# A two-layer hybrid mixer on one core: the output tiles of the local and latent attention are turned two jobs behind their products instead of one

## The chip, the cores and the metric

The kernel runs on one core of one Trainium2 chip. The metric is the time of the device in microseconds (us) for one execution; lower is better. The median of three runs stands for a kernel.

Engines are named as in the profile: PE is TensorE (the matrix engine; PEld is its loading of weights), DVE is VectorE, ACT is ScalarE, POOL is GpSimd, SP is SyncE. PSUM is the memory that PE writes its products to, in eight banks; the program calls it `ps`.

## The reference, cut to what matters

Two layers over 512 latent tokens and 256 context tokens of width 1024. Each layer multiplies the normed tokens by one wide matrix, runs four token mixers side by side (local attention "a", an mLSTM "b", latent attention "c", differential attention "d"), and merges them by gates:

```python
def merge_branches(ys, gate_logits, w_branch, w_out):
    g = jax.nn.sigmoid(gate_logits.reshape(gate_logits.shape[:2] + (N_BRANCH, D_MODEL)))
    merged = sum(g[:, :, i] * (y @ w_branch[i]) for i, y in enumerate(ys))
    return merged @ w_out
```

The local attention has 8 heads of width 64, a window of 128 tokens on either side and the context; the latent attention has 4 heads of width 128 and sees all tokens. In both, per block of 128 query tokens and per head:

```python
p_win, p_ctx = joint_softmax([jnp.where(valid, score(qg, k_win), -jnp.inf), score(qg, k_c)], sink_f)
return values(p_win, v_win) + values(p_ctx, v_c)
```

A gated feed-forward network closes each layer. In the second layer only the latent tokens are still needed.

## The kernel before

The program is one long sequence of phases; each engine has its own stream of instructions, written by hand, and semaphores join them. Most phases are big matrix products in which every weight and every activation is split in a high and a low part (`w_hi`, `w_lo`, `u_hi`, `u_lo`), so that three matmuls stand for one.

**An attention phase** (`attend`, once for PE, once for ACT, once for DVE) works through a list of jobs. A job is one block of 128 query tokens and one head; a token block is called a tile, and its jobs follow one another: 8 in "a", 4 in "c" and "d". The first layer has 6 tiles and the second 4. Job `i` goes: scores on PE (L1433, L1439, masks L1447; written for two jobs at a time in "a" and "c", at odd `i`); maxima on DVE (L2742, L2745 or L2748); exponentials on ACT (L2032, L2034); the probabilities are transposed on PE (`probs_t`, L1467) into banks 4 and 5; ACT copies bank 4 out (L2045) and DVE bank 5 (L2784); the product with the values on PE (`values`, L1481); and DVE scales its result into `y_tok` (`y_copy`, L2795).

**Turning an output tile** (`tile_t`, L1493): when all heads of a tile are in `y_tok`, PE transposes its four 128x128 blocks into bank 4, the bank that the transposed probabilities use too. ACT then copies the bank to `y_hi` (`yt_copy`, L2070; L2068 in "d"), and DVE writes the rest to `y_lo` (`yt_low`, L2732; L2729 in "d"). Until that is done, the next `probs_t` may not write bank 4:

```python
if n.yt:
    pe.wait_ge(yt_copied, n.yt)
```

**Filling**: between these steps PE works on the product of another matrix (the gates' weights), whose matmuls are L1404: three for each 128x128 block of weights, 384 columns wide in the first layer and 512 in the second. They are what PE does while it would wait. How many stand in each job is a table written by hand (`FillPlan`; first of each pair for the first layer, second for the second layer). Of it, the local and the latent attention:

```python
THREE, FOUR, LONG = [8, 8, 8], [6, 6, 6, 6], [12, 12, 24]
"a": (3 * THREE + [12, 6, 6] + THREE + [6, 6, 12] + 2 * THREE + [6, 12, 6] + 2 * THREE + [12, 6, 6] + THREE +
      [6, 6, 12] + THREE + [4, 4],
      2 * FOUR + [5, 9, 5, 5] + FOUR + [5, 9, 5, 5] + FOUR + [5, 9, 5, 5] + [5, 4, 4]),
"c": ([24, 12, 12, 12, 12, 24] + LONG + [24] + THREE + [24] + LONG + [24] + THREE + [24, 16],
      [14, 10, 12, 12, 10, 14] + THREE + [14, 10, 7, 7, 10, 16]),
```

In "a" and "c", an odd job `i` runs on PE as: scores of `i+1` and `i+2`, values of `i-1`, perhaps a turn, all of its fill, `probs_t(i)`. An even job runs as: half of its fill (rounded down), values of `i-1`, perhaps a turn, the other half, `probs_t(i)`. In "d" every job is of the first kind, with one job's scores. The fill's chunks of 24 matmuls use bank 7 one after the other, and ACT evicts each (L2018). The weights of the fill are split while the jobs run (L2007 on ACT, L2717 on DVE).

Of the kernel before, what the change touches and what calls it, by code (L numbers as in the profile page):

```python
# [324 lines left out]
def build(nc, x, c, ctx_in, c_ctx, w_mod, b_mod, g_mix_pre, g_mix_post, g_ffn_pre, g_ffn_post, w_in, a_sink,  # L325
# [4 lines left out]
    with stack:  # L330
# [578 lines left out]
        def _(pe):  # L909
# [501 lines left out]
            def attend(l, kind, g):  # L1411
# [84 lines left out]
                    n.yt += 1  # L1496

                map0, job0 = n.map, n.job
                late = 2 if kind == "d" else 1
                scores(0)  # L1500
                for i in range(len(jobs)):
                    final = i + 1 == len(jobs)
# [119 lines left out]
            for index, (kind, l, arg) in enumerate(phases):  # L1622
                if kind == "gemm":
                    gemm(arg, background.get(index))
                elif kind == "opening":
                    opening(phases[index + 1][2][0])
                    continue
                elif kind == "close":
                    close(l, arg, phases[index + 1][2])
                    continue  # L1630
                elif kind.startswith("prep_"):
                    transposes(v_blocks(kind, l))
                elif kind == "mlstm":
                    mlstm(l, arg)
                elif kind == "attend":
                    attend(l, *arg)
                onward = kind in ("gemm", "mlstm", "attend") and phases[index + 1][0] in ("gemm", "close")
                ph.end_products(onward)
# [3 lines left out]
        def _(act):  # L1642
# [347 lines left out]
            def attend(l, kind, g):  # L1990
# [80 lines left out]
                    n.yt += 1  # L2071

                yt0 = n.yt
                late = 2 if kind == "d" else 1
                yt_tiles = [jobs[i][0] for i in range(heads - 1, len(jobs), heads)]
                evicted = 0
                exps(0)
# [108 lines left out]
            for index, (kind, l, arg) in enumerate(phases):  # L2186
                if kind == "gemm":
                    gemm(l, arg, phases[index + 1][2])
                elif kind == "opening":
                    opening(phases[index + 1][2][0])  # L2190
                elif kind == "close":
                    close(l, arg, phases[index + 1][2][0])
                elif kind.startswith("prep_"):
                    blocks = v_blocks(kind, l)
                    for i, (srcs, t) in enumerate(blocks):
                        act.wait_ge(tr_ready, n.tr + 1)
                        bank = ps[:, 4 + n.tr % 2, :]
                        if kind == "prep_a":
                            A(av_tok[:, t, :], bank[:, 0:P], ACT.Copy).then_inc(tr_copied, 1)
                        else:  # L2200
                            A(v_tok[:, t, :], bank, ACT.Copy).then_inc(tr_copied, 1)
                        n.tr += 1
                elif kind == "mlstm":
                    mlstm(l, arg)
                elif kind == "attend":
                    attend(l, *arg)
                ph.end()
# [3 lines left out]
        def _(dve):  # L2211
# [486 lines left out]
            def attend(l, kind, g):  # L2698
# [1 line left out]
                heads = A_HEADS if kind == "a" else HEADS  # L2700
                dv = 64 if kind == "a" else HD
                map0, job0, yt0 = n.map, n.job, n.yt
                late = 2 if kind == "d" else 1
                yt_tiles = [jobs[i][0] for i in range(heads - 1, len(jobs), heads)]
                plan = FillPlan(l, kind)

# [254 lines left out]
            for index, (kind, l, arg) in enumerate(phases):  # L2961
# [27 lines left out]
                elif kind == "opening":  # L2989
                    opening(phases[index + 1][2][0])  # L2990
                elif kind == "close":
                    close(l, arg, phases[index + 1][2][0])
                elif kind.startswith("prep_"):
                    n.tr += len(v_blocks(kind, l))
                elif kind == "mlstm":
                    mlstm(l, arg)
                elif kind == "attend":
                    attend(l, *arg)
# [175 lines left out]
```

## Time and profile before

| | |
|---|---|
| median of 3 runs | 3251.06 us (3247.45 to 3252.42) |
| the profiled execution's own time | 3253.5 us |
| its span in the trace | 3251.6 us |
| PE matmuls busy | 3137.8 us (97% of the span) |
| DVE busy | 1685.2 us (52%) |
| ACT busy | 1151.1 us (35%) |
| mean granted PE clock | 0.994 |

The profile is one execution. PE is the engine to watch: what makes it stand still, or adds to its work, is added to the time unless something later takes it back.

### The profile page before, as it was taken

How to read it: one execution, taken by the hardware profiler on the slowest of the kernel's cores; microseconds unless marked ns; L12 is line 12 of the kernel's file. 1: busy time of each engine (PE TensorE's matmuls, PEld its weight loads, DVE VectorE, ACT ScalarE, POOL GpSimd, SP SyncE). 2: the span in 40 equal slices, each digit the busy share in tenths (PEclk: the TensorE clock that was granted, in tenths of full speed). 3: DMA queues.
4: the chain of work that ended last, by engine and by line, in shares of the span. 5: the costliest groups of instructions: out<-in, count | busy, mean ns of one | idle time of the engine just before them, and what ended most of it. 6: DMA issues, size and time to landing. Idle time of an engine off the chain costs nothing. (4 is left out here: it accounts for less than half of the span.)

```text
span 3251.6 us, 46215 instructions
## 1 busy us (share of the span) xinstructions
PE 3137.8 (97%) x18246; PEld 2833.2 (87%) x18246; DVE 1685.2 (52%) x3126; ACT 1151.1 (35%) x1961; POOL 225.4 (7%) x184
## 2 busy tenths in 40 slices
PE   8999999999999999999999999999999999899999
PEld 6999988998898789999999988778877887788887
DVE  5645455333366866753222575545444578565234
ACT  4233344333313444322212433334343235442223
POOL 1001100100020010000000010110100110100000
PEclk9999999999999999999999999999999999999999
DMA  8312410320241124531221552141321521353423
GB/s 289 120 34 66 134 42 14 130 65 27 78 163 61 32 78 136 162 113 54 74 65 58 158 164 79 63 132 31 113 65 40 182 71 40 130 154 90 113 82 105
DMA packets 353232, 309.31 MB, mean 95 GB/s; under 512 B 40639, under 2 KB 329357, under 8 KB 351757
## 3 DMA queue, kind: packets, MB, share of 16 engines
q1 hardware_dynamic: 331022, 240.65, 24.7%
q10 hardware_dynamic: 22014, 65.99, 5.5%
q8 instruction: 132, 2.16, 0.3%
q14 instruction: 64, 0.52, 0.0%
HBM read 272.89 MB, written 33.29 MB: 94 GB/s over the span
## 5 line engine op out<-in xcount | busy, mean ns | idle before, releaser
L1045 PE MATMUL ps<-u_hi,w_hi 128*128 128x384 f32 (+1 forms) x2040 | 588.9, 351 | 5.8 <-issue 3.0
L1045 PE MATMUL ps<-u_hi,w_lo 128*128 128x384 f32 (+1 forms) x2040 | 583.1, 348 | 0.0
L1045 PE MATMUL ps<-u_lo,w_hi 128*128 128x384 f32 (+1 forms) x2040 | 583.0, 348 | 0.0
L2221 DVE TENSOR_TENSOR w_lo<-w_raw,w_hi 128x2048 fp32r<-128x2048 f32 x129 | 297.8, 2309 | 349.6 <-ACT w_hi L1654 347.0
L1045 PEld LDWEIGHTS ps<-u_hi,w_hi 128*128 128x128 f32 x2040 | 369.6, 188 | 28.2 <-issue 7.2
L1045 PEld LDWEIGHTS ps<-u_hi,w_lo 128*128 128x128 f32 x2040 | 372.9, 188 | 18.7
L1045 PEld LDWEIGHTS ps<-u_lo,w_hi 128*128 128x128 f32 x2040 | 372.7, 188 | 18.0
L1404 PE MATMUL ps<-u_hi,w_hi 128*128 128x384 f32 (+1 forms) x816 | 307.6, 377 | 6.0 <-ACT space L2018 3.7
L1654 ACT ACTIVATE w_hi<-w_raw 128x2048 fp32r<-128x2048 f32 x129 | 246.1, 1907 | 149.3 <-issue 68.7
L1404 PE MATMUL ps<-u_hi,w_lo 128*128 128x384 f32 (+1 forms) x816 | 296.7, 364 | 0.0
L1404 PE MATMUL ps<-u_lo,w_hi 128*128 128x384 f32 (+1 forms) x816 | 294.0, 360 | 0.0
L2479 DVE SCALAR_TENSOR_TENSOR space<-space,silu_c 128x256 f32<-128x256 f32 x574 | 253.9, 484 | 10.4
L1708 ACT ACTIVATE space<-ps 128x768 f32<-128x768 f32 (+3 forms) x102 | 76.7, 752 | 500.3 <-PE ps L1045 492.6
L1481 PEld LDWEIGHTS ps<-space 128*128 128x128 f32 x1472 | 179.5, 192 | 37.6 <-DVE space L2784 16.0
L2742 DVE TENSOR_REDUCE mx<-ps 128x1 f32<-128x768 f32 (+3 forms) x200 | 156.2, 781 | 101.7 <-PE ps L1439 75.0
L1481 PE MATMUL ps<-space 128*128 128x128 f32 (+1 forms) x1472 | 197.8, 280 | 6.6 <-DVE space L2784 5.3
L1404 PEld LDWEIGHTS ps<-u_hi,w_hi 128*128 128x128 f32 x816 | 154.7, 190 | 21.9 <-issue 7.1
L2254 DVE TENSOR_TENSOR space<-space,ps 128x768 f32<-128x768 f32 (+1 forms) x44 | 36.1, 821 | 251.3 <-PE ps L1045 243.3
L1404 PEld LDWEIGHTS ps<-u_hi,w_lo 128*128 128x128 f32 x816 | 154.3, 189 | 9.5
L1404 PEld LDWEIGHTS ps<-u_lo,w_hi 128*128 128x128 f32 x816 | 154.8, 190 | 8.3
L2034 ACT ACTIVATE space<-ps,nmx 128x768 f32<-128x768 f32 (+3 forms) x160 | 119.2, 745 | 72.6 <-DVE nmx L2748 70.7
L1439 PE MATMUL ps<-space 64*128 64x256 f32 (+2 forms) x784 | 130.3, 450 | 15.1 <-ACT space L2034 12.5
(307 smaller groups left out, 5121.1 us busy)
## 6 DMA issues: line engine op xcount, KB each, us to landing
w_raw<-in_w_in SPq DMA_DIRECT2D x288, 256.0 KB, 3.8
w_raw<-in_w_gate_up SPq DMA_DIRECT2D x176, 256.0 KB, 3.9
space<-in_w_mod SPq DMA_DIRECT2D x40, 1024.0 KB, 5.3
w_raw<-in_w_down SPq DMA_DIRECT2D x114, 192.0 KB, 2.9
w_raw<-in_w_branch SPq DMA_DIRECT2D x64, 256.0 KB, 3.5
w_raw<-in_w_out SPq DMA_DIRECT2D x48, 256.0 KB, 3.8
m_scratch<-space ACTq DMA_DIRECT2D x3, 3072.0 KB, 10.0
space<-m_scratch ACTq DMA_DIRECT2D x3, 3072.0 KB, 10.3
```

Of the source, the lines that this page charges most:

```text
L1045: last = nc.tensor.matmul(ps[:, 2 * (t % 2) + b, 0:a1 - a0], wv[w][:, k, j * P:(j + 1) * P], xx[:, k, a0:a1], start=(k == 0 and w == 0 and ...
L1404: last = nc.tensor.matmul(ps[:, fill_bank, 0:cols.stop - cols.start], wv[w][:, k, j * P:(j + 1) * P], xx[:, k, cols], start=k == 0 and m = ...
L1439: last = nc.tensor.matmul(ps[:, 2 * slot + at // 512, at % 512:at % 512 + b - a], lhs, rhs(a, b), start=not deep, stop=not here)
L1481: last = nc.tensor.matmul(ps[:, 6, h * dv:(h + 1) * dv], pt_buf[i % 2][:, bi * P:(bi + 1) * P], v, start=bi == 0, stop=bi == len(keys) - 1)
L1654: A(w_hi[slot][:, :], w_raw[slot][:, :], ACT.Copy).then_inc(w_hi_done, 1)
L1708: A(tile_at(dst_tile(g, it, s, j), g.lat), acc_of(g, it, s, j, t), ACT.Copy if g.kind == "copy" else ACT.Sigmoid, scale=HD ** -0.5 if g.na ...
L2034: A(p_slot(kind, n.map)[:, 0:w], view, ACT.Exp, bias=nmx[:, n.map % 4:n.map % 4 + 1], scale=c_scale[:, t:t + 1] if kind == "c" else SCALE[ ...
L2221: V.tensor_tensor(w_lo[slot][:, :], w_raw[slot][:, :], w_hi[slot][:, :].bitcast(F32), ALU.subtract).then_inc(w_lo_done, 1)
L2254: V.tensor_tensor(tile_at(30 + s, g.lat), tile_at(30 + s, g.lat), acc(t % 2, g.lat), ALU.mult).then_inc(hid_ready, 1)
L2479: ins = V.scalar_tensor_tensor(part[:, sg], w, silu_c[:, k, sg:sg + 1], part[:, sg], ALU.mult, ALU.add)
L2742: own.did(V.reduce_max(mx[:, c4:c4 + 1], view, AX))
```

## The change

`late` says how many jobs after a tile's last job its turn stands. It was 2 for the differential attention and 1 for the others; now it is 2 for all. On PE the turn moves from job `heads*k + 1` to job `heads*k + 2`, on ACT and DVE the copies move with it. No instruction is added or removed. A phase's last tile is turned behind its last job, as before. So 16 turns move: 5 in "a" and 5 in "c" of the first layer, 3 and 3 in the second.

```diff
@@ -1496,7 +1496,7 @@
                 map0, job0 = n.map, n.job
-                late = 2 if kind == "d" else 1
+                late = 2
                 scores(0)
@@ -2071,7 +2071,7 @@
                 yt0 = n.yt
-                late = 2 if kind == "d" else 1
+                late = 2
                 yt_tiles = [jobs[i][0] for i in range(heads - 1, len(jobs), heads)]
@@ -2700,7 +2700,7 @@
                 map0, job0, yt0 = n.map, n.job, n.yt
-                late = 2 if kind == "d" else 1
+                late = 2
                 yt_tiles = [jobs[i][0] for i in range(heads - 1, len(jobs), heads)]
```

What stands on PE in the second layer's local attention around the first turn, before the change; from the turn (L1493) to the next transposed probabilities (L1467) there are nine matmuls of the fill:

```order
L1493 MATMUL ps<-ident,space 128x128 [waits y_copied]
L1493 MATMUL ps<-ident,space 128x128 x3
L1404 MATMUL ps<-u_hi,w_lo 128x512
L1404 MATMUL ps<-u_hi,w_hi 128x512
L1404 MATMUL ps<-u_lo,w_hi 128x512
L1404 MATMUL ps<-u_hi,w_lo 128x512
L1404 MATMUL ps<-u_hi,w_hi 128x512
L1404 MATMUL ps<-u_lo,w_hi 128x512
L1404 MATMUL ps<-u_hi,w_lo 128x512
L1404 MATMUL ps<-u_hi,w_hi 128x512
L1404 MATMUL ps<-u_lo,w_hi 128x512
L1467 MATMUL ps<-ident,space 128x128 [waits yt_copied,pt_copied,probs_ready]
```

And the same turn after the change, one job later:

```order
L1481 MATMUL ps<-space 128x64 [waits pt_copied]
L1481 MATMUL ps<-space 128x64 x4
L1493 MATMUL ps<-ident,space 128x128 [waits y_copied]
L1493 MATMUL ps<-ident,space 128x128 x3
L1404 MATMUL ps<-u_lo,w_hi 128x512
L1404 MATMUL ps<-u_hi,w_lo 128x512
L1404 MATMUL ps<-u_hi,w_hi 128x512
L1467 MATMUL ps<-ident,space 128x128 [waits yt_copied,pt_copied,probs_ready]
```

The turn has moved behind the next job's values, and three fill matmuls are left between it and the transposed probabilities.

On ACT at the same place before, the copy of the turned tile (L2070) stands behind the exponentials (L2034) of the next job:

```order
L2032 ACTIVATE esink<-sink,nmx 128x1 [waits pt_ready,max_ready]
L2034 ACTIVATE space,den<-ps,nmx 128x640
L2070 ACTIVATE y_hi<-ps 128x4x128 [waits yt_ready]
L2045 ACTIVATE space<-ps 128x384 [waits pv_ready,pt_ready]
L2032 ACTIVATE esink<-sink,nmx 128x1 [waits pt_ready,max_ready]
```

And after:

```order
L2045 ACTIVATE space<-ps 128x384 [waits pv_ready,pt_ready]
L2032 ACTIVATE esink<-sink,nmx 128x1 [waits pt_ready,max_ready]
L2034 ACTIVATE space,den<-ps,nmx 128x640
L2070 ACTIVATE y_hi<-ps 128x4x128 [waits yt_ready]
L2045 ACTIVATE space<-ps 128x384 [waits pv_ready,pt_ready]
```

The copy has moved behind one copy of probabilities and one pair of exponentials more, and is again the last before a copy of probabilities.

## Rows read from the trace of the kernel before

**Rows 1.** The page: busy time of the engines.

```profile
PE 3137.8 (97%) x18246; PEld 2833.2 (87%) x18246; DVE 1685.2 (52%) x3126; ACT 1151.1 (35%) x1961; POOL 225.4 (7%) x184
```

**Rows 2.** Waits of PE, whole span: total us, times, longest.

```profile
PE ps L1481 <- DVE space L2784: 5.3, 9, 1.1
...
PE ps L1404 <- ACT space L2018: 3.7, 11, 0.6
...
PE ps L1467 <- DVE y_lo L2729: 2.8, 3, 1.5
```

**Rows 3.** Timeline, first layer's "a", a turn: start us, us, engine, line, instruction.

```profile
475.94 0.61 PE L1493 MATMUL ps<-ident,space 128*128 128x128 f32 x4
...
476.30 0.42 PE L1404 MATMUL ps<-u_hi,w_hi 128*128 128x384 f32 x1
...
476.94 0.19 ACT L2034 ACTIVATION_READ_ACCUMULATOR space<-ps,nmx 128x1 f32 x1
477.03 0.58 ACT L2070 ACTIVATE y_hi<-ps 128x512 fp32r<-128x512 f32 x1
...
477.64 0.69 DVE L2732 TENSOR_TENSOR y_lo<-ps,y_hi 128x512 fp32r<-128x512 f32 x1
...
478.50 0.61 PE L1467 MATMUL ps<-ident,space 128*128 128x128 f32 x4
```

**Rows 4.** Timeline, the job behind it, where the turn goes.

```profile
480.18 0.20 ACT L2034 ACTIVATION_READ_ACCUMULATOR space<-ps,nmx 128x1 f32 x1
480.87 0.42 PE L1404 MATMUL ps<-u_lo,w_hi 128*128 128x384 f32 x1
...
481.17 0.28 DVE L2795 TENSOR_SCALAR space<-ps,rden 128x64 f32<-128x64 f32 x1 [1.33 <-PE ps L1481]
...
481.65 0.60 PE L1467 MATMUL ps<-ident,space 128*128 128x128 f32 x4
```

**Rows 5.** Timeline, the last turn of the same phase.

```profile
593.22 0.60 PE L1493 MATMUL ps<-ident,space 128*128 128x128 f32 x4
...
593.86 0.60 ACT L2070 ACTIVATE y_hi<-ps 128x512 fp32r<-128x512 f32 x1 [2.44 <-PE ps L1493]
...
594.49 0.69 DVE L2732 TENSOR_TENSOR y_lo<-ps,y_hi 128x512 fp32r<-128x512 f32 x1 [1.48 <-ACT y_hi L2070]
```

**Rows 6.** Timeline, first layer's "c", a new place of a turn.

```profile
841.89 1.05 ACT L2007 ACTIVATE w_hi<-w_raw 128x1024 fp32r<-128x1024 f32 x1
...
842.54 0.42 PE L1404 MATMUL ps<-u_lo,w_hi 128*128 128x384 f32 x1
```

**Rows 7.** Timeline, PE, new places: first layer's "c", second layer's "a".

```profile
869.03 0.42 PE L1404 MATMUL ps<-u_hi,w_lo 128*128 128x384 f32 x1
...
870.51 0.82 PE L1467 MATMUL ps<-ident,space 128*128 128x128 f32 x6
...
2230.46 0.48 PE L1404 MATMUL ps<-u_lo,w_hi 128*128 128x512 f32 x1
2230.78 0.40 PE L1404 MATMUL ps<-u_hi,w_lo 128*128 128x512 f32 x1
...
2231.24 0.71 PE L1467 MATMUL ps<-ident,space 128*128 128x128 f32 x5
```

**Rows 8.** Timeline, differential attention, waits behind a turn of both layers.

```profile
1165.41 0.74 DVE L2729 SCALAR_TENSOR_TENSOR y_lo<-ps,g_sub,y_hi 128x512 fp32r<-128x512 f32 x1
...
1166.30 0.84 PE L1467 MATMUL ps<-ident,space 128*128 128x128 f32 x6 [1.50 <-DVE y_lo L2729]
...
2736.50 0.85 PE L1467 MATMUL ps<-ident,space 128*128 128x128 f32 x6 [1.01 <-DVE y_lo L2729]
```

**Rows 9.** Busy time by stretch: PE, PEld, DVE, ACT, POOL, then granted clock, DMA.

```profile
1160.00:1168.40 8.40, 6.25 (x45) 5.73 (x44) 7.16 (x15) 3.16 (x6) 0.00 (x0) 1.00 0.38 127
1168.50:1171.80 3.30, 3.30 (x17) 3.30 (x16) 1.35 (x3) 0.33 (x1) 0.00 (x0) 0.50 0.00 0
...
2735.00:2740.00 5.00, 3.99 (x28) 2.62 (x27) 3.86 (x10) 2.36 (x6) 0.00 (x0) 1.00 0.00 0
```

## The prediction

> **What bounds the kernel now.** I read the page first: PE's matmuls are busy for 3137.8 of 3251.6 us [rows 1], so whatever lengthens PE's own stream or makes it stand still is paid, and work taken off another engine is not. The change touches only when PE turns a tile, so the next view is what PE waits for, and there the column to look at is the releaser. The transposes of the probabilities (L1467) wait for `y_lo` three times in the whole kernel, 2.8 us together, and each time for line 2729, which is the differential attention's: the attention that turns two jobs behind [rows 2]. For line 2732, the same copy in the local and latent attention, no such row exists. The turns that this change moves cost PE no wait today.
>
> Why they cost none is to be seen in the timeline around one of them [rows 3]. The turn starts on PE at 475.94; its copy to `y_hi` is taken up by ACT at 477.03, because ACT is first busy with exponentials until then, and DVE ends `y_lo` at 477.64 + 0.69 = 478.33. PE comes to its next transposed probabilities at 478.50. Between lie the 12 fill matmuls that the table gives to this job. So the cover is just enough: 0.17 us to spare in the local attention. It is good to keep in mind that it was made for this place: in all five turns of this phase the table has 12 in the job of the turn, and 6 or 8 in the next.
>
> **What is removed and added.** No instruction comes or goes. Three things move by one job: on PE four transposes, on ACT one copy, on DVE one subtraction. What changes is the order, and with it what lies between a turn and the probabilities that may not be written before `y_lo` is done.
>
> *The length of the chain.* From the turn's start to the earliest start of the next `probs_t`, with ACT and DVE free, the last turn of the same phase shows it link by link [rows 5]: turn starts 593.22, ACT starts 593.86 (0.64 later), DVE starts 594.49 (0.63 later), DVE ends 595.18 (0.69 later). From the end of DVE's copy to PE's start the differential attention shows 1165.41 + 0.74 = 1166.15 to 1166.30, that is 0.15 [rows 8]. Sum: 0.64 + 0.63 + 0.69 + 0.15 = 2.11 us. It is shorter than the old one, where ACT came 0.45 later (1.09 from start to start instead of 0.64) [rows 3].
>
> *Are ACT and DVE free at the new place?* In the job behind the turn of rows 3, ACT ends its exponentials at 480.38, and the turn, which would take the slot of the first fill matmul at 480.87 and lasts 0.60, would end at 481.47. DVE scales the values' result from 481.17 to 481.45, and is wanted for `y_lo` only at 480.87 + 1.27 = 482.14 [rows 4]. The tightest place is one of the latent attention, where ACT splits weights until 841.89 + 1.05 = 842.94, and the turn would end at 842.54 + 0.60 = 843.14 [rows 6]. So both are free, and 2.11 stands for all places.
>
> *What covers it now.* The turn itself keeps PE's queue moving for 0.36 us (475.94 to 476.30) [rows 3]; that piece is only moved. Then comes half of an even job's fill. Four matmuls of 384 columns take 481.65 - 480.87 = 0.78 [rows 4], eight take 870.51 - 869.03 = 1.48 [rows 7], so one more costs 0.175, three take 0.61 and six take 1.13. Of 512 columns three take 2231.24 - 2230.46 = 0.78; the first takes 0.32, the other two 0.23 each [rows 7], so four take 1.01, five 1.24, eight 1.93.
>
> *The wait at each of the 16 places* is 2.11 - 0.36 - fill, or 1.75 - fill. The fill's count is the second half of the table's entry at job `heads*k + 2`:
> - first layer, local: 3, 4, 3, 3, 4 matmuls: 3 x 1.14 + 2 x 0.97 = 5.36
> - first layer, latent: 6, 4, 6, 4, 8: 2 x 0.62 + 2 x 0.97 + 0.27 = 3.45
> - second layer, local: 3, 3, 3 wide ones: 3 x 0.97 = 2.91
> - second layer, latent: 4, 5, 8 wide ones: 0.74 + 0.51 + 0 = 1.25
>
> Together 12.97 us in 15 waits. A start after a wait is slightly dearer: six transposes take 0.85 behind a wait [rows 8] and 0.82 in the flow [rows 7], so 15 x 0.03 = 0.45 more. Sum 13.4 us.
>
> *What it buys.* At the old place PE waits for nothing, so there is nothing to get back there: the exponentials in front of ACT's copy cost PE nothing. At most, the copies of probabilities and the evictions come up to one copy sooner in odd jobs. PE waits for those (L2784 and L2018) 5.3 + 3.7 = 9.0 us in the whole kernel [rows 2], which bounds that gain from above; nothing bounds it away from zero. I take 0, since in an odd job ACT and DVE have already ended the turned tile before `probs_t` begins, and the copy of the probabilities starts only behind it. What is queued behind the new wait is, on PE, the transposes and the two jobs' scores; ACT and DVE wait for these and have nothing else to be late with, so they move with PE and are no second cost.
>
> *Sum.* 3253.5 + 13.4 = 3266.9 us against the profiled execution, which lies 2.4 us above the median; against the median, **3264.5 us**.
>
> *The clock.* The granted clock was 1.00 up to 1168.4 and 0.50 from 1168.5 to 1171.8, just behind the 1.50 us wait at 1166.30; it stayed at 1.00 around the 1.01 us wait at 2736.50 [rows 8, 9]. So waits of this kind can take PE to 1.2 GHz and did so once. The trace ends a matmul about 0.16 us after the next could issue (0.34 recorded, 0.175 apart), so my waits will show as idle times of 0.8 to 1.0 us, nearer to the one that did no harm. By the rows I add nothing. The Trainium skill, "TensorE: Matmul & The Clock Gate", section "A second HAM failure mode: psum-queue depth-cycling", speaks against me here: it tells of a kernel whose small idle times between groups of matmuls, repeated often, made the clock go back and forth. By that rule the sum would be that of rival 1; of the two waits that I can show in the differential attention, one agrees with it and one doesn't.
>
> **The rivals.**
> 1. *The new waits also cost clock.* A stretch at half clock of 3.3 us [rows 9] loses 1.65 us. If each of the ten waits of 0.97 us or more brought one, that is 16.5 us: 3253.5 + 13.4 + 16.5 = 3283.4, or 3281 by the median. For it: 1166.30. Against: 2736.50, and that ten waits would all have to do what about one in two did at 1.0 to 1.5 us. It decides from idle times of some 1.5 us on. A single fall or two are in my own range.
> 2. *The waits are there, but are given back.* A PE that comes later finds its later operands ready. All that there is to give back of this kind are the 9.0 us of rows 2, and that is the whole kernel with the differential attention and both tails: 3253.5 + 13.4 - 9.0 = 3257.9, or 3255.5 by the median, no difference that one could tell. Against: these waits hang on PE's own products one or two steps before, and so move with it.
> 3. *Faster.* The turn's copies leave the odd job, in which ACT and DVE do two jobs' exponentials and maxima, for the even job, which has little; copies of probabilities and evictions come sooner, and the 9.0 us go: 3253.5 - 9.0 = 3244.5, or 3242 by the median. It needs the chain to fit into 0.36 + 0.61 to 0.78, about 1.0 to 1.1 us, where it decides; the trace says 2.11, half of it.
>
> **How the numbers follow.** My forecast has 0.86, rival 1 0.05, rival 2 (or a wait that I have misread, with no visible difference) 0.07, rival 3 0.02. What can be told from no change by a measurement of this kernel is about 0.2%, or 6.5 us: below 3244.6 is faster, above 3257.6 slower. My forecast's own range: each link of the chain is good to 0.15 us, 15 x 0.15 = 2.3; two falls of the clock are 3.3 more; the median itself moves by some 2.5; half of rival 2's give-back is 4.5 less. That makes 3258 to 3270.5, and leaves out about 2 in 10 with the rivals. Slower 0.88, same 0.09, faster 0.03.
>
> **What the profile of the changed kernel would show.** PE's waits get a new row, L1467 for L2732, about 15 times and 10 to 11 us in total (13.0 less 0.16 for each), the longest about 1.0, none in the last turn of a phase. In the timeline ACT's copy of a turned tile starts 0.04 us after the turn's end, no longer 0.45. PE's busy time stays within a few us. The waits for L2784 and L2018 stay near 5.3 and 3.7. Wrong I would be if `probs_t` found `y_lo` done (the chain shorter than 2.11), if that row is there but the span has not grown by as much (rival 2), or if the granted clock shows new stretches of 0.50 in the four attentions (rival 1).

## The result

| | before | changed |
|---|---|---|
| median | 3251.51 us (6 runs, 3247.45 to 3252.42) | 3264.79 us (6 runs, 3263.37 to 3266.25) |
| the profiled execution's own time | 3253.5 us | 3263.37 us |
| its span | 3251.6 us | 3261.5 us |
| PE matmuls busy | 3137.8 us | 3141.1 us |
| mean granted PE clock | 0.994 | 0.994 |

The change makes the kernel slower: the ratio is 1.0042, with a 95% interval of 1.0030 to 1.0055, that is 9.8 to 17.9 us. The medians lie 13.3 us apart. The forecast was 3264.5.

The same view as in [rows 2], what PE waits for, now has a row that was not there. Its columns are total us, times and the longest:

```profile
PE ps L1467 <- DVE y_lo L2732: 10.4, 14, 1.0
...
PE ps L1045 <- DVEq L2306: 5.6, 7, 1.4
PE ps L1481 <- DVE space L2784: 5.3, 9, 1.1
...
PE ps L1404 <- ACT space L2018: 3.8, 11, 0.6
...
PE ps L1467 <- DVE y_lo L2729: 1.3, 2, 1.0
```

The transposes of the probabilities wait 14 times for the copy to `y_lo` in the local and latent attention. The rows of L2784 and L2018 are as they were, so nothing was given back there. The row of the differential attention (L2729) is smaller; more on it below.

The timeline of the changed kernel at the turn of [rows 3 and 4], now one job later:

```profile
482.45 0.20 ACT L2034 ACTIVATION_READ_ACCUMULATOR space<-ps,nmx 128x1 f32 x1
483.16 0.61 PE L1493 MATMUL ps<-ident,space 128*128 128x128 f32 x4
483.44 0.28 DVE L2795 TENSOR_SCALAR space<-ps,rden 128x64 f32<-128x64 f32 x1 [1.33 <-PE ps L1481]
483.52 0.42 PE L1404 MATMUL ps<-u_lo,w_hi 128*128 128x384 f32 x1
...
483.81 0.60 ACT L2070 ACTIVATE y_hi<-ps 128x512 fp32r<-128x512 f32 x1 [1.16 <-PE ps L1493]
...
484.13 0.33 PE L1404 MATMUL ps<-u_lo,w_hi 128*128 128x384 f32 x1
484.44 0.69 DVE L2732 TENSOR_TENSOR y_lo<-ps,y_hi 128x512 fp32r<-128x512 f32 x1 [0.72 <-ACT y_hi L2070]
485.28 0.63 PE L1467 MATMUL ps<-ident,space 128*128 128x128 f32 x4 [0.81 <-DVE y_lo L2732]
```

From the turn's start at 483.16 to the transposes at 485.28 it is 2.12 us, against 2.11 in the prediction. PE's last fill matmul starts at 484.13, so the next could have started at about 484.31, and 0.97 us are lost; the trace calls 0.81 of it idle, since it ends that matmul at 484.46.

How much a whole phase grew is read between two marks on PE in the same kernel: the first transposed probabilities of the first layer's local attention, and its last turn.

```profile
432.16 0.69 PE L1467 MATMUL ps<-ident,space 128*128 128x128 f32 x2
...
600.30 0.60 PE L1493 MATMUL ps<-ident,space 128*128 128x128 f32 x4
```

That is 168.14 us. In the kernel before, whose last turn is in [rows 5], the first mark is this one:

```profile
430.66 0.66 PE L1467 MATMUL ps<-ident,space 128*128 128x128 f32 x2
```

So it was 593.22 - 430.66 = 162.56 us. The phase grew by 5.58 us; the prediction had 5.36 for it, and 0.15 for the dearer starts. The same two marks can be read in the other three phases. The latent attention of the first layer took 142.48 us (735.74 to 878.22) and now takes 146.07 (742.77 to 888.84). The local attention of the second layer took 120.19 (2193.36 to 2313.55) and now takes 123.18 (2201.56 to 2324.74), and the latent attention there took 102.89 (2427.06 to 2529.95) and now takes 104.24 (2438.03 to 2542.27). The four phases grew by 5.58, 3.59, 2.99 and 1.35 us, 13.5 together.

### The profile page after: what moved, and what is told of

Its sections match the earlier page's. It is cut to its first block and busy times, and to the rows that moved or that the text cites. A ratio compares the mean times of both kernels' runs of the same rounds, so it can differ in the third digit from the quotient of the medians.

```text
span 3261.5 us, 46215 instructions
## 1 busy us (share of the span) xinstructions
PE 3141.1 (96%) x18246; PEld 2833.5 (87%) x18246; DVE 1684.7 (52%) x3126; ACT 1153.0 (35%) x1961; POOL 225.0 (7%) x184
## 5 line engine op out<-in xcount | busy, mean ns | idle before, releaser
L1045 PEld LDWEIGHTS ps<-u_hi,w_lo 128*128 128x128 f32 x2040 | 372.3, 188 | 18.7
L2479 DVE SCALAR_TENSOR_TENSOR space<-space,silu_c 128x256 f32<-128x256 f32 x574 | 253.8, 484 | 10.4
L2784 DVE COPY space<-ps 128x256 f32<-128x256 f32 (+2 forms) x160 | 72.1, 451 | 143.2 <-PE ps L1467 142.7
```

What stands on the lines that cost most here:

```text
L1045: last = nc.tensor.matmul(ps[:, 2 * (t % 2) + b, 0:a1 - a0], wv[w][:, k, j * P:(j + 1) * P], xx[:, k, a0:a1], start=(k == 0 and w == 0 and ...
L2479: ins = V.scalar_tensor_tensor(part[:, sg], w, silu_c[:, k, sg:sg + 1], part[:, sg], ALU.mult, ALU.add)
L2784: V.tensor_copy(pt_buf[i % 2][:, w0:w], ps[:, 5, 0:w - w0]).then_inc(pt_copied, 1)
```

## The experiments

All are compared with the kernel before in runs on the same chip; the ratio of each is to those runs, and its interval is the 95% one. A ratio is not exactly the quotient of the two medians; where the difference matters, both are given.

**One attention at a time.** The change in the local attention alone, in all three places:

```diff
-                late = 2 if kind == "d" else 1
+                late = 1 if kind == "c" else 2
```

> Only the local attention turns two jobs behind; the latent attention stays at one. Theory (the wait is the chain of 2.11 us less 0.36 and less the fill behind the turn): eight turns move, 5.36 us in the first layer and 2.91 in the second, with the dearer starts 8.5 us more than before, about 3260.0; PE's waits for line 2732 are 8, some 7 us in total. Rival (the clock pays too, or the places help each other): the sum of the two single kernels differs from the whole change's 13.3 by over 3 us.

Measured: 3260.66 us against 3249.52 of before, ratio 1.0028 (1.0016 to 1.0040). And in the latent attention alone:

```diff
-                late = 2 if kind == "d" else 1
+                late = 1 if kind == "a" else 2
```

> Only the latent attention turns two jobs behind; the local attention stays at one. Theory: eight turns move, 3.45 us in the first layer and 1.25 in the second, with the dearer starts 4.9 us more than before, about 3256.4; seven waits for line 2732, the longest 0.8, and the sums of both single kernels make the 13.3 of the whole change. Rival (a fixed price of each moved turn, whatever the fill): the same as the local attention's, 6.6 us each.

Measured: 3255.65 us against 3249.52, ratio 1.0018 (1.0009 to 1.0027). By the ratios that is 9.1 and 5.9 us, together 15 against 13.7 by the ratio of the whole change. By the medians it is 11.1 and 6.1, together 17 against 13.3, which is more than the 3 us apart that were set for the rival in the first of these two. With an interval of some 4 us on either side for the local kernel and 3 for the latent one, these times decide neither that nor between 5.9 and the second rival's 6.6; the traces do. Between the marks used above, the four phases grew by 8.45 us in the local kernel and 5.0 in the latent one, together the 13.5 of the whole change, and by no more than 0.1 in a phase whose turns did not move. First the local, then the latent kernel, what PE waits for:

```profile
PE ps L1467 <- DVE y_lo L2732: 7.0, 8, 1.0
```

```profile
PE ps L1467 <- DVE y_lo L2732: 3.5, 6, 0.8
```

Eight turns moved in each, with 7.0 and 3.5 us of idle time: not a fixed price for a moved turn, and together, to 0.1 us, the 10.4 of the whole change. The seventh wait of the latent attention, behind eight fill matmuls, is too short for this view; in the change it is the 0.09 us between the end of this fill matmul at 881.02 and the transposes:

```profile
880.68 0.34 PE L1404 MATMUL ps<-u_hi,w_hi 128*128 128x384 f32 x1
881.11 0.63 PE L1467 MATMUL ps<-ident,space 128*128 128x128 f32 x4
```

**The cover moved along.** This is the experiment that decides between the place and the cover. The turns are two jobs behind as in the change, but in the table the job of the turn has at least 10 fill matmuls, taken from its neighbours where it had fewer (in the first layer's local attention it gets the 12 that the job ahead of it had), and the job of the turn puts all but three of its fill matmuls behind the turn. That leaves 9 or 13 behind a turn, and 7 in the second layer's local attention, where the expectation says 8 at least:

```diff
-        "a": (3 * THREE + [12, 6, 6] + THREE + [6, 6, 12] + 2 * THREE + [6, 12, 6] + 2 * THREE + [12, 6, 6] + THREE +
-              [6, 6, 12] + THREE + [4, 4],
-              2 * FOUR + [5, 9, 5, 5] + FOUR + [5, 9, 5, 5] + FOUR + [5, 9, 5, 5] + [5, 4, 4]),
-        "c": ([24, 12, 12, 12, 12, 24] + LONG + [24] + THREE + [24] + LONG + [24] + THREE + [24, 16],
-              [14, 10, 12, 12, 10, 14] + THREE + [14, 10, 7, 7, 10, 16]),
+        "a": (3 * THREE + [6, 12, 6] + 2 * THREE + [12, 6, 6] + THREE + [6, 6, 12] + 2 * THREE + [6, 12, 6] +
+              2 * THREE + [12, 6, 6] + [4, 4],
+              2 * FOUR + [5, 4, 10, 5] + FOUR + [5, 4, 10, 5] + FOUR + [5, 4, 10, 5] + [5, 4, 4]),
+        "c": ([24, 12, 12, 12, 12, 24] + LONG + [24] + [12, 6, 6] + [24] + LONG + [24] + [12, 6, 6] + [24, 16],
+              [14, 10, 12, 12, 10, 14] + [12, 6, 6] + [12, 12, 7, 7, 10, 16]),
...
-                late = 2 if kind == "d" else 1
+                late = 2
...
+                    turns = i > late and (i - late) % heads == 0
+                    ahead = 0 if scored or final else 3 if turns and kind != "d" else plan.quota[i] // 2
...
-                        fill(plan.quota[i] - (0 if scored else plan.quota[i] // 2))
+                        fill(plan.quota[i] - ahead)
```

> Two jobs behind as in the change, but the fill is moved along: in the table the job of the turn gets what the job ahead of it had (totals per chunk as before), and a job with a turn puts 3 fill matmuls ahead of its values and the rest, 8 to 13, behind the turn. Theory (it is only the cover that counts, not the place): nine matmuls of 384 columns cover 1.66 of the 1.75 us, the wide ones all of it; waits for line 2732 under 1 us in total, time 3252 to 3253, 12 of the 13.3 us given back. Rival (the place is bad by itself, because ACT and DVE stand otherwise there): the waits or the time stay, 3258 or more.

Measured: 3250.61 us against 3249.52, ratio 1.0000 (0.9991 to 1.0009). The loss is gone within the interval of 2.9 us on either side, with the turns at the same place as in the change. The rival's 3258 or more is excluded. Between the marks used above, the four phases of this kernel take 1.7 us more than before, instead of 13.5. The same turn in its timeline (the lines of this kernel are two higher from here on):

```profile
481.26 0.61 PE L1493 MATMUL ps<-ident,space 128*128 128x128 f32 x4
481.54 0.28 DVE L2797 TENSOR_SCALAR space<-ps,rden 128x64 f32<-128x64 f32 x1 [1.15 <-PE ps L1481]
481.63 0.42 PE L1404 MATMUL ps<-u_hi,w_hi 128*128 128x384 f32 x1
...
481.91 0.60 ACT L2072 ACTIVATE y_hi<-ps 128x512 fp32r<-128x512 f32 x1 [0.98 <-PE ps L1493]
...
482.54 0.69 DVE L2734 TENSOR_TENSOR y_lo<-ps,y_hi 128x512 fp32r<-128x512 f32 x1 [0.72 <-ACT y_hi L2072]
...
483.10 0.34 PE L1404 MATMUL ps<-u_hi,w_lo 128*128 128x384 f32 x1
483.38 0.63 PE L1467 MATMUL ps<-ident,space 128*128 128x128 f32 x4
```

ACT starts 0.65 and DVE 1.28 us behind the turn's start, the same chain as in the change. Only what PE does meanwhile is different: nine fill matmuls from 481.63 on, and the transposes start at 483.38, 2.12 behind the turn with at most 0.1 us lost. In its waits no row for this copy is left; what is left of the kind is the differential attention's:

```profile
PE ps L1467 <- DVE y_lo L2731: 1.3, 2, 1.0
```

**The cover taken from the old place.** The kernel before, turns one job behind, with that table and nothing else changed (the diff is the table's above).

> One job behind as before the change, but with the table of the kernel with moved cover, so the old place has 6 or 8 fill matmuls instead of 12 in the local attention of the first layer and 4 instead of 9 in that of the second; the latent attention keeps 10 to 24 there. Theory: the old chain is 2.54 us (ACT's copy waits for exponentials), less 0.36, less a fill of 1.13, 1.48 or 1.01: 1.05, 0.70, 1.05, 1.05, 0.70 and three times 1.14, with the dearer starts 8.2 us more than before, 3259.7, all of it in the local attention. Rival (the old place needs no cover): the time of before, 3251.5.

Measured: 3258.45 us against 3251.0, ratio 1.0020 (1.0011 to 1.0029), that is 6.5 us with an interval of 3.6 to 9.4 (7.5 by the medians). The time is below the 8.2 expected and does not exclude it; the waits agree closely, eight, and 6.5 us of idle time where 7.97 less 0.16 for each makes 6.7:

```profile
PE ps L1467 <- DVE y_lo L2732: 6.5, 8, 1.0
```

So the old place needs its fill as the new one does. But not all of these waits reach the time: between the marks the four phases grew by only 5.6 us in this trace, and the first local attention by 2.7, where its five waits alone were expected to cost 4.6. The fill that is taken from the job of the turn stands in other jobs; what it saves there is not shown by any row that I have.

**One link of the chain made shorter.** The change, with only the first of the four blocks of the copy ahead of the release. The other three blocks of `y_lo` are written as zeros behind it, so this kernel leaves out three quarters of the low part:

```diff
-                        V.tensor_tensor(lo, src, hi, ALU.subtract).then_inc(yt_copied, 1)
+                        if j + 1 < len(yt_tiles):
+                            V.tensor_tensor(lo[:, 0:1, :], src[:, 0:1, :], hi[:, 0:1, :],
+                                            ALU.subtract).then_inc(yt_copied, 1)
+                            V.tensor_tensor(lo[:, 1:4, :], hi[:, 1:4, :], hi[:, 1:4, :], ALU.subtract)
+                        else:
+                            V.tensor_tensor(lo, src, hi, ALU.subtract).then_inc(yt_copied, 1)
```

> As the change, but DVE's copy that releases PE covers one block of 128 columns instead of 512; the other three blocks of y_lo are written as zeros from SBUF behind the release (left out: three quarters of y_lo in all turns but a phase's last, in the local and latent attention). Theory: that link of the chain falls from 0.69 to about 0.33 us, and every wait with it: 14 times 0.36 and once 0.27 less, so 5.3 us of the 13.4 are given back, 3259.6; the waits for line 2732 (now its own line) last 0.6 where they lasted 1.0. Rival (PE waits for ACT's copy or for something else behind it): no change, 3264.8.

Measured: 3260.02 us against 3251.0, ratio 1.0026 (1.0015 to 1.0037): 8.5 us, with an interval of 4.9 to 12.0, where 8.1 were expected. That the whole change's 13.3 lie outside it does not decide alone, since the change has an interval of its own from 9.8 on. The trace decides. Its timeline at the first turn:

```profile
460.96 0.60 ACT L2070 ACTIVATE y_hi<-ps 128x512 fp32r<-128x512 f32 x1 [0.57 <-PE ps L1493]
461.11 0.34 PE L1404 MATMUL ps<-u_hi,w_lo 128*128 128x384 f32 x1
461.59 0.29 DVE L2733 TENSOR_TENSOR y_lo<-ps,y_hi 128x128 fp32r<-128x128 f32 x1 [0.72 <-ACT y_hi L2070]
461.79 0.55 DVE L2735 TENSOR_TENSOR y_lo<-y_hi 128x384 fp32r<-128x384 f32 x1
462.02 0.41 PE L1467 MATMUL ps<-ident,space 128*128 128x128 f32 x2 [0.58 <-DVE y_lo L2733]
```

The link lasts 0.29 instead of 0.69, and PE starts 0.14 behind its end. The wait follows the link one for one: idle 0.58, where the change has 0.98 at this turn, in this row of its timeline:

```profile
460.38 0.41 PE L1467 MATMUL ps<-ident,space 128*128 128x128 f32 x2 [0.98 <-DVE y_lo L2732]
```

In the view of waits, the row of the kernel with the short link is down to this:

```profile
PE ps L1467 <- DVE y_lo L2733: 4.7, 11, 0.6
```

That is 5.7 us less than the 10.4 of the change. The time follows too: from the first turn to the last one of this phase, five waits apart, it is 140.00 us (460.31 to 600.31) where the change takes 142.03 (458.27 to 600.30), five times 0.41.

**Three jobs behind.** On the table of before:

```diff
-                late = 2 if kind == "d" else 1
+                late = 2 if kind == "d" else 3
```

> Three jobs behind in the local and latent attention, on the table of before. The turn is again in an odd job, with all of that job's fill behind it and exponentials ahead of ACT's copy, but the last moved turn of the latent attention comes into the phase's last job, which has no fill. Theory: chain 2.54 (local) or 2.34 (latent), less 0.36, less fills of 6, 8, 8, 6, 8 (local, first layer: 4.2 us), 12, 8, 12, 8, none (latent: 2.8), 5, 5, 5 wide ones (2.7), 8, 7, none (2.1): 11.8 us, with dearer starts 12.2, so 3263.7, no later than the change. Rival (each job that a turn is late costs the same again): 3278.

Measured: 3262.0 us against 3251.0, ratio 1.0037 (1.0023 to 1.0051), 12.0 us where 12.2 were expected, with an interval of 7.5 to 16.6 that excludes the rival's 3278. Being a job later still costs nothing more. At the place without any fill the chain stands bare in the timeline:

```profile
878.63 0.60 PE L1493 MATMUL ps<-ident,space 128*128 128x128 f32 x4
...
879.27 0.60 ACT L2070 ACTIVATE y_hi<-ps 128x512 fp32r<-128x512 f32 x1 [2.20 <-PE ps L1493]
879.90 0.69 DVE L2732 TENSOR_TENSOR y_lo<-ps,y_hi 128x512 fp32r<-128x512 f32 x1 [0.64 <-ACT y_hi L2070]
880.74 0.85 PE L1467 MATMUL ps<-ident,space 128*128 128x128 f32 x6 [1.50 <-DVE y_lo L2732]
```

878.63 to 880.74 is 2.11 us, the sum of the prediction measured in one piece.

The time agrees better than its parts. At the first moved turn of the latent attention the formula has no wait, since twelve fill matmuls stand behind the turn. There is one of 0.52, since ACT was still busy with exponentials and took up its copy 1.78 us behind the turn's start, where it is 0.88 or 0.89 at the next three:

```profile
769.68 0.60 PE L1493 MATMUL ps<-ident,space 128*128 128x128 f32 x4
...
771.37 0.19 ACT L2034 ACTIVATION_READ_ACCUMULATOR space<-ps,nmx,c_scale 128x1 f32 x1
771.46 0.59 ACT L2070 ACTIVATE y_hi<-ps 128x512 fp32r<-128x512 f32 x1
...
772.92 0.41 PE L1467 MATMUL ps<-ident,space 128*128 128x128 f32 x2 [0.52 <-DVE y_lo L2732]
```

On the other side PE waits less for the evictions (L2018):

```profile
PE ps L1467 <- DVE y_lo L2732: 9.7, 13, 1.5
...
PE ps L1404 <- ACT space L2018: 2.7, 8, 0.6
```

In the kernel before that row is 3.7 us, so 1.0 us was given back here, as rival 2 of the prediction has it, while in the change itself nothing was. Between the marks the four phases of this kernel grew by 10.3 us, not 12.2; what makes up the rest of the difference is not shown.

None of these kernels beats the one before: the best of them, with the cover moved along, is level with it. At the old place the chain is covered already, so neither another place nor a shorter chain has a wait to take away there.

## Why the prediction was right

*The length of the chain*, 2.11 us: measured 2.10 to 2.12 at the fifteen places of the change where PE waits, and 2.11 bare, three jobs behind.

*ACT and DVE are free at the new place*: ACT's copy starts 0.04 us after the turn's end (483.77 to 483.81) with the engine idle ahead of it for 1.16 us, and DVE's starts 0.03 us behind ACT's end. At all 16 places of the change ACT starts 0.64 or 0.65 us behind the turn's start.

*The wait is 1.75 less the fill*: of the sixteen places, 14 have a wait in the view, one has 0.09 us and one has none, as predicted. The predicted 12.97 us less 0.16 for each of 15 make 10.6; the trace has 10.4 and 0.09. With the old place's longer chain (2.54 in the local attention) the formula also gives the waits of cover taken and those of cover moved; three jobs behind it misses one of the 16 places, where ACT was not free. The kernel with moved cover shows that the cover is not only needed but enough.

*What it buys is nothing*: the rows of L2784 and L2018 are 5.3 and 3.8, before 5.3 and 3.7.

*One reading was off, without effect on the sum.* The prediction gives the old place 0.17 us to spare, from DVE's end at 478.33 to PE's start at 478.50 [rows 3]. But PE starts 0.15 behind DVE's end even when it waits for it, by the prediction's own link [rows 8]. So what was to spare is 0.02 us: the old chain is 2.54 us, as at the same turn in the kernel with the cover taken (479.30 to 481.84), and PE came 2.56 us behind the turn. The table is exact to the last matmul here.

*The sum*, 13.4 us on the profiled execution: the medians differ by 13.3. With an interval of 9.8 to 17.9 us, an agreement to 0.1 is partly luck. The phases say more: by the prediction's terms, with 0.03 for each start, they should grow by 5.51, 3.60, 3.00 and 1.31 us, and they grew by 5.58, 3.59, 2.99 and 1.35. The one profiled span grew by only 9.9, and here the forecast would have seemed 3.5 too high to whoever had only the two spans. The 3.6 us by which the rest of the span got shorter are outside the four phases; the largest piece is a row that was this in the kernel before:

```profile
PE ps L1045 <- DVEq L2306: 8.3, 7, 3.6
```

In the changed kernel's trace it is 5.6, with 1.4 the longest, 2.7 us less. It is 6.9 and 6.8 in the two kernels with one attention changed, and 7.2 three jobs behind, so it moves from execution to execution or with the alignment of phases; I have no run that says which. The row of the differential attention (L2729) is 1.3 instead of 2.8 and likewise 1.3 or 2.8 in the others.

*Rival 1, the clock*, is not borne out. The stretches of the changed kernel that hold the 16 moved turns, with the granted clock in the third column from the end:

```profile
440.00:600.00 160.00, 152.62 (x1106) 135.06 (x1105) 88.17 (x286) 71.16 (x202) 0.00 (x0) 1.00 0.09 27
750.00:890.00 140.00, 135.90 (x818) 113.14 (x817) 52.56 (x123) 44.00 (x88) 0.00 (x0) 1.00 0.10 31
2225.00:2325.00 100.00, 95.34 (x671) 78.48 (x669) 55.77 (x164) 45.41 (x112) 0.00 (x0) 1.00 0.10 33
2465.00:2545.00 80.00, 78.27 (x443) 59.85 (x442) 32.76 (x66) 26.20 (x45) 0.00 (x0) 1.00 0.10 31
```

It is 1.00 throughout. Nor did the clock take more elsewhere: read in slices of 1 us, both traces have nine stretches of lower clock while PE works, and the sum of 1 less the granted clock over them is 18.7 us in both. So the oscillation that the Trainium skill describes in "TensorE: Matmul & The Clock Gate", section "A second HAM failure mode: psum-queue depth-cycling", does not occur with waits of up to 1 us here; the trace disagrees with it as a forecast for this kernel. That rival 1 would decide from idle times of some 1.5 us on is not borne out either: three jobs behind, two waits of 1.50 us brought no fall (last section). *Rival 2* falls for the change by the same rows as the gain, *rival 3* by the sign.

## What to carry to other kernels

Where PE fills the time of a round trip through two other engines with work from a table, the place of the step and the table are one decision: moving the step by one job without its entries exposed 1.75 us less whatever fill happened to stand there, in 15 of 16 places. The price can be worked out before building: measure the chain once where nothing covers it, count what PE has left between the step and the next use of its bank, and subtract. It must be looked up at every place whether the other engines are free: three jobs behind, one busy ACT gave a wait where none was due. The view of waits tells that there is no wait, but not how near one is. That is told only by the timeline, and the way from the last copy's end to PE has to be taken off too: of 0.17 us here, 0.02 were left.

## What the runs showed of the hardware

A wait of 1.50 us need not cost clock. Before, one was followed two microseconds later by a stretch at 0.50 [rows 8, 9], with another wait of 0.65 us in between, at 1167.79; three jobs behind, the wait of 1.50 us shown above was followed by none, and neither was another of 1.50 at 2534. That the fall at 1168.5 came from the wait ahead of it, as the prediction reads it, is therefore not shown. The rows:

```profile
878.00:886.00 8.00, 6.50 (x51) 6.26 (x49) 1.95 (x4) 1.58 (x3) 0.00 (x0) 1.00 0.42 133
2531.00:2540.00 9.00, 7.50 (x52) 6.62 (x52) 3.73 (x7) 1.78 (x4) 0.00 (x0) 1.00 0.00 0
```

And the same program text can go either way. Behind the same wait of 3.4 us at the start of the first mLSTM phase, ahead of everything that the change touches, the kernel before had its full clock and the changed one had half of it, 1.2 GHz, in this order:

```profile
180.60:183.80 3.20, 3.20 (x20) 3.17 (x19) 2.09 (x11) 0.00 (x0) 0.00 (x0) 1.00 0.02 5
```

```profile
180.60:183.80 3.20, 3.20 (x12) 3.11 (x11) 2.09 (x11) 0.00 (x0) 0.00 (x0) 0.50 0.02 5
```

Twelve matmuls were recorded in these 3.2 us instead of twenty. Single executions of one kernel here lie up to 12 us apart (3243.83 to 3255.84 in 22 runs of the kernel before). Such stretches seem to be the main source of it: the mean granted clock of the fastest of these runs was 0.996 and that of the slowest 0.992, and 0.004 of 3250 us is 13 us, by my estimate. That is why changes of this size need medians, or the same two marks in both traces, and not the span of one trace.
